# The inverse of the delta rule in blocks of 64 tokens on two quadrants of TensorE

## The reference

```python
def chunk_gated_delta(q, k, v, beta, g):      # CHUNK = 64, 4 heads, dk = dv = 128
    ...
    L = jnp.where(strict, jnp.einsum('bhnid,bhnjd->bhnij', kb, k) * gamma, 0.0)
    rhs = jnp.concatenate([v * beta[..., None], kb * jnp.exp(gc)[..., None]], axis=-1)
    sol = lax.linalg.triangular_solve(jnp.eye(C, dtype=L.dtype) + L, rhs,
                                      left_side=True, lower=True, unit_diagonal=True)
    U, W = sol[..., :dv], sol[..., dv:]
```

## Time and profile before

| | us |
|---|---|
| median of 3 runs (lowest, highest) | 1252.11 (1249.11, 1254.0) |
| the profiled execution, its own time | 1254.81 |
| its span, first to last instruction | 1253.0 |
| PE busy in the span | 1182.9 |
| DVE busy in the span | 671.5 |
| ACT busy in the span | 557.8 |
| mean granted TensorE clock, share of full | 0.982 |

### The profile page before, as it was taken

The page is one execution under the profiler, slowest core; times in us unless marked ns, Lnnn a source line. Parts: engine busy times, 40 slices in busy tenths (PEclk is TensorE's granted clock), DMA queues, the critical chain, the costliest instruction groups (busy, mean ns, idle before and its releaser), DMA issues.

```text
span 1253.0 us, 15678 instructions
## 1 busy us (share of the span) xinstructions
PE 1182.9 (94%) x6279; PEld 876.6 (70%) x6279; DVE 671.5 (54%) x720; ACT 557.8 (45%) x633; POOL 46.2 (4%) x90
## 2 busy tenths in 40 slices
PE   5999989999998999889998999999999989999986
PEld 5989868888887977677844848638658458477351
DVE  4866665444454433478804857408668048484053
ACT  3771344343434376356704636307447046354041
POOL 7000000000000022000000000000000000000000
PEclk8999999999998999989999999999999999999999
DMA  9622139655553432248989999999999899998993
GB/s 313 181 101 69 35 123 379 223 199 170 189 178 131 153 135 75 86 144 317 331 325 421 419 420 421 367 421 420 417 384 419 329 421 419 410 413 318 421 417 125
DMA packets 116926, 352.07 MB, mean 281 GB/s; under 512 B 8096, under 2 KB 55216, under 8 KB 116848
## 3 DMA queue, kind: packets, MB, share of 16 engines
q1 hardware_dynamic: 115552, 347.11, 72.2%
q0 software_dynamic: 1296, 3.90, 1.0%
HBM read 349.93 MB, written 1.05 MB: 280 GB/s over the span
## 4 chain that ended last, share of the span: by engine, by line
PE 85%; DMA 6%; DVE 5%; ACT 3%; issue 1%; SPq 0%; DVEq 0%; ACTq 0%
PE ps L547 20%; PE ps L548 19%; PE ps L549 19%; PE ps L1584 8%; PE ps L1605 6%; DMA arena_c<-in_o_moe_w_dram 4%; PE ps L1529 2%; PE ps L1566 2%; DVE all_lo L1755 1%; DMA arena_a<-in_o_moe_w_dram 1%; PE ps L1541 1%; PE ps L1290 1%; DMA arena_a<-in_e_w_in_dram 1%; PE ps L1448 1%; PE ps L1285 1%
## 5 line engine op out<-in xcount | busy, mean ns | idle before, releaser
L1755 DVE TENSOR_TENSOR all_lo<-arena_c,all_hi 128x1408 fp32r<-128x1408 f32 (+1 forms) x120 | 170.7, 1448 | 215.8 <-ACT all_hi L794 215.5
L794 ACT ACTIVATE all_hi<-arena_c 128x1408 fp32r<-128x1408 f32 (+1 forms) x120 | 146.5, 1247 | 242.9 <-DMA arena_c<-in_o_moe_w_dram 196.9
L1755 DVE TENSOR_TENSOR all_lo<-arena_a,all_hi 128x1408 fp32r<-128x1408 f32 (+1 forms) x96 | 138.4, 1471 | 23.8 <-ACT all_hi L794 23.4
L547 PE MATMUL ps<-all_hi,xg_hi 128*128 128x512 f32 (+1 forms) x384 | 145.2, 378 | 2.9 <-ACT u_act L1037 2.9
L548 PE MATMUL ps<-all_lo,xg_hi 128*128 128x512 f32 (+1 forms) x384 | 144.4, 376 | 0.0
L794 ACT ACTIVATE all_hi<-arena_a 128x1408 fp32r<-128x1408 f32 (+1 forms) x96 | 119.2, 1262 | 55.1 <-PE ps L549 35.2
L549 PE MATMUL ps<-all_hi,xg_lo 128*128 128x512 f32 (+1 forms) x384 | 143.7, 374 | 0.0
L547 PE MATMUL ps<-all_hi,x_hi 128*128 128x512 f32 (+1 forms) x336 | 126.2, 376 | 4.2 <-DVE all_lo L1748 2.3
L1748 DVE TENSOR_TENSOR all_lo<-arena_a,all_hi 128x2048 fp32r<-128x2048 f32 x40 | 91.4, 2290 | 62.1 <-ACT all_hi L787 62.1
L548 PE MATMUL ps<-all_lo,x_hi 128*128 128x512 f32 (+1 forms) x336 | 122.9, 366 | 0.0
L549 PE MATMUL ps<-all_hi,x_lo 128*128 128x512 f32 (+1 forms) x336 | 122.7, 365 | 0.0
(11 more groups left out here) (350 smaller groups left out, 1820.6 us busy)
## 6 DMA issues: line engine op xcount, KB each, us to landing
arena_c<-in_o_moe_w_dram SPq DMA_DIRECT2D x136, 704.0 KB, 9.3
arena_a<-in_o_moe_w_dram SPq DMA_DIRECT2D x120, 704.0 KB, 9.0
arena_c<-in_o_moe_w_dram SPq DMA_DIRECT2D x45, 1024.0 KB, 14.5
arena_a<-in_o_moe_w_dram SPq DMA_DIRECT2D x35, 1024.0 KB, 15.6
arena_c<-in_e_ffn_w_dram SPq DMA_DIRECT2D x36, 512.0 KB, 4.8
arena_a<-in_e_ffn_w_dram SPq DMA_DIRECT2D x30, 512.0 KB, 5.1
arena_a<-in_e_w_in_dram SPq DMA_DIRECT2D x24, 512.0 KB, 8.8
arena_a<-in_o_w_qkv_dram SPq DMA_DIRECT2D x12, 512.0 KB, 4.2
```

The lines of the kernel that those rows point to most:

```text
L547: pe.matmul(o, a_hi, b_hi, start=first, stop=False)
L794: act.activation(unit(all_hi, st), in_ring(WHERE[v][0] + off, st.size), ACT.Copy).then_inc(hi_done, 1)
L1755: tt(unit(all_lo, st), in_ring(WHERE[v][0] + off, st.size), unit(all_hi, st).bitcast(F32), ALU.subtract).then_inc(lo_done, 1)
```

## The change

Levels 0 to 5 never connect the first 64 tokens of a unit with the last 64, so X, X transposed and T are block diagonal until level 6. The change keeps only the two 64x64 diagonal blocks, each on its own partitions, packed to 64 columns per unit. Every matmul of 128x128x128 becomes two of 64x64x64: one with rows 0 to 63 of the array into partitions 0 to 63, one with rows 64 to 127 into partitions 64 to 127 of the same bank. DVE's instructions shrink from 128x512 to 128x256. At level 5 the last subtraction writes the two blocks into `inv_all`, 128 columns per unit, with one instruction for each half of the partitions. The last level becomes two corner products per unit, with a plain copy and a multiplication by -1 on DVE, 64 partitions each. `inv_all` then takes the place of `inv_xt` in the solve. POOL copies the masks into packed form once the convolution no longer needs the memory, and sets the unused corner of `inv_all` to zero; it builds one mask less at the start. The fillers keep their places.

```diff
-    LEVELS = 7
+    LEVELS = 6
...
+            pool.wait_ge(conv_done, 6)
+            for rows in HALVES:
+                pool.tensor_copy(half_masks[rows, 0:LEVELS, :], level[rows, 0:LEVELS, rows])
+                pool.tensor_copy(half_masks[rows, LEVELS, :], ident[rows, rows])
+            pool.memset(inv_all[HALVES[1], :, HALVES[0]], 0.0)
+            pool.drain().then_inc(masks_ready, 1)
...
+            def in_halves(bank, hf, a, b):
+                for m in range(4):
+                    u = 4 * hf + m
+                    for rows in HALVES:
+                        last = mm(ps[rows, bank, m * CH:(m + 1) * CH], a(u, rows), b(u, rows), start=True, stop=True)
+                return last
...
-                    for m in range(4):
-                        u = 4 * hf + m
-                        last = mm(ps[:, hf, m * P:(m + 1) * P], lower[:, u, :], inv_x[:, u, :] if k else ident[:, :],
-                                  start=True, stop=True)
-                    last.then_inc(t_done, 1)
+                    in_halves(hf, hf, lambda u, rows: lower[rows, u, rows], x_part_of if k else unit_of).then_inc(t_done, 1)
+                fill(k)
...
-                    if 0 < k < LEVELS - 1:
...
+                        in_halves(6 + hf, hf, xt_part_of, t_part_of).then_inc(x_done, 1)
+                    in_halves(2 + hf, hf, t_part_of, xt_part_of if k else unit_of).then_inc(xt_done, 1)
+            first, second = HALVES
+            for hf in range(2):
+                pe.wait_ge(x_ready, 2 * LEVELS + hf - 1)
+                for m in range(4):
+                    u = 4 * hf + m
+                    last = mm(ps[second, hf, m * CH:(m + 1) * CH], lower[first, u, second], inv_x[first, u, :], start=True, stop=True)
+                last.then_inc(t_done, 1)
+            fill(LEVELS)
+            for hf in range(2):
+                pe.wait_ge(t_ready, 2 * LEVELS + hf + 1)
+                pe.wait_ge(xt_ready, 2 * LEVELS + hf - 1)
+                for m in range(4):
+                    u = 4 * hf + m
+                    last = mm(ps[first, 2 + hf, m * CH:(m + 1) * CH], inv_t[second, u, :], inv_all[second, u, second],
+                              start=True, stop=True)
+                last.then_inc(xt_done, 1)
             gate_mix()
...
-                last = mm(two(0)[:, u * P:(u + 1) * P], kbe[:, u, :], inv_xt[:, u, :], start=True, stop=True)
+                last = mm(two(0)[:, u * P:(u + 1) * P], kbe[:, u, :], inv_all[:, u, :], start=True, stop=True)
...
+            vec.wait_ge(masks_ready, 1)
             for k in range(LEVELS):
...
-                    tt(inv_t[:, us, :], ps[:, hf, :].rearrange("p (u n) -> p u n", u=4), units4(level[:, k, :]),
-                       ALU.mult).then_inc(t_ready, 1)
+                    tt(inv_t[:, us, :], units_of(hf), units4(half_masks[:, k, :]), ALU.mult).then_inc(t_ready, 1)
...
+                    if k < LEVELS - 1:
+                        tt(inv_xt[:, us, :], old_xt, units_of(2 + hf), ALU.subtract).then_inc(xt_ready, 1)
+                    else:
+                        for rows in HALVES:
+                            ins = tt(inv_all[rows, us, rows], old_xt[rows], units_of(2 + hf)[rows], ALU.subtract)
+                        ins.then_inc(xt_ready, 1)
...
+            for hf in range(2):
+                us = slice(4 * hf, 4 * hf + 4)
+                vec.wait_ge(t_done, 2 * LEVELS + hf + 1)
+                vec.tensor_copy(inv_t[second, us, :], units_of(hf)[second]).then_inc(t_ready, 1)
+            for hf in range(2):
+                us = slice(4 * hf, 4 * hf + 4)
+                vec.wait_ge(xt_done, 2 * LEVELS + hf + 1)
+                ts(inv_all[first, us, second], units_of(2 + hf)[first], -1.0, None, ALU.mult).then_inc(xt_ready, 1)
             gate_out()
```

More of the change, by code:

```diff
@@ L275, in trunk @@
         level_at = nc.sbuf_base
-        level = sb("level", [P, LEVELS, P])
+        level = sb("level", [P, LEVELS + 1, P])
         iota = sb("iota", [P, P])
@@ L315, in trunk @@
         rows_raw = kd[:, 0, :]
[L316 to L318 removed]
+        inv_at = conv_in[:, :, :].rearrange("p a b -> p (a b)")
+        inv_x, inv_xt, inv_t = (inv_at[:, k * U * CH:(k + 1) * U * CH].rearrange("p (u n) -> p u n", u=U) for k in range(3))
+        inv_all = inv_at[:, 3 * U * CH:3 * U * CH + U * P].rearrange("p (u n) -> p u n", u=U)
+        half_at = 3 * U * CH + U * P
+        half_masks = inv_at[:, half_at:half_at + (LEVELS + 1) * CH].rearrange("p (k n) -> p k n", n=CH)
+        HALVES = (slice(0, CH), slice(CH, P))
         vb = xn[:, 0, :].rearrange("p (u n) -> p u n", u=U)
@@ L392, in trunk @@
         back = put("back", [SLOTS, TILES, P])
-        assert end[0] <= level_at + 4 * LEVELS * P
+        assert end[0] <= level_at + 4 * (LEVELS + 1) * P
         y_exp = over(gain_at + 4 * D)[0]("y_exp", [SLOTS, D])
@@ L1274, in _, with x_part_of, xt_part_of, t_part_of @@
                     (project_N if i < 10 else project_T)(i, 4 + i % 2, [half])
+            def in_halves(bank, hf, a, b):
[4 more added lines that the diff above has]
+                return last
+            def x_part_of(u, rows):
+                return inv_x[rows, u, :]
+            def xt_part_of(u, rows):
+                return inv_xt[rows, u, :]
+            def t_part_of(u, rows):
+                return inv_t[rows, u, :]
+            def unit_of(u, rows):
+                return ident[rows, rows]
+            for k in range(LEVELS):
+                for hf in range(2):
+                    if k:
+                        pe.wait_ge(x_ready, 2 * k + hf - 1)
+                    in_halves(hf, hf, lambda u, rows: lower[rows, u, rows], x_part_of if k else unit_of).then_inc(t_done, 1)
+                fill(k)
                 if k == 0:
@@ L1296, in _ @@
             for u in range(U):
-                last = mm(two(0)[:, u * P:(u + 1) * P], kbe[:, u, :], inv_xt[:, u, :], start=True, stop=True)
+                last = mm(two(0)[:, u * P:(u + 1) * P], kbe[:, u, :], inv_all[:, u, :], start=True, stop=True)
             last.then_inc(sol_done, 1)
             for u in range(U):
-                last = mm(two(6)[:, u * P:(u + 1) * P], inv_xt[:, u, :], vb[:, u, :], start=True, stop=True)
+                last = mm(two(6)[:, u * P:(u + 1) * P], inv_all[:, u, :], vb[:, u, :], start=True, stop=True)
```

24 lines of the change are left out of this document (11 added, 13 removed).

## The result

The changed kernel takes 1240.13 us (median of 4 runs, 1238.94 to 1241.57) beside 1253.05 for the kernel before (4 runs, 1249.11 to 1255.54): a ratio of 0.9902, 95% interval 0.9887 to 0.9917. The prediction was 1239.5. The profiled execution took 1240.6, with a span of 1238.6.

What follows compares the result with a forecast made beforehand. PE's instruction stream was taken as the bound: 13.2 + 1.8 - 2.1 - 0.3 = 12.6 us less, giving 1242.2 profiled or 1239.5 as median. Forecast's own range 1236.5 to 1242.5, over the cases 1236.5 to 1252.

Steps and rivals of the forecast that it cites:

- PE's stream is the bound and what it saves counts in full: Inverse, 84 to 142 us: PE busy 55.8 of 58 us, so its savings count in full while DVE keeps up.
- A pair in 0.060: Two 64x64x64 records on opposite quadrants take 0.060 us, so 16 groups save 0.83 each, 13.2 us in all.
- The changes of tiling, 0.30 a stretch: Seven tiled stretches on PE's path, each about 0.30 us more for switching tiling; 2.1 us lost.
- The seventh stretch: XT of the last level, in front of `gate_mix`; charged about 0.30 us for tiling like the other stretches.
- The first stretch: XT of level 0 with T of level 1; charged about 0.30 us for changing the tiling.
- The change of tiling into the scores: Existing row-tiled scores: 0.85 us less 0.64 for slots at full overlap, so a tiling change costs 0.2.
- The last level on one quadrant, 0.89 each: Last level's T and XT: 16 unpaired records each at 0.056, 0.89 us saved each, 1.8 together.
- T of level 0 hidden by the wait for `kbe`: T of level 0 would end earlier, but PE then waits for ACT's `kbe` until 87.87 anyway; no gain counted.
- DVE keeps pace; 0.3 for the waits: Inverse: DVE instructions fall to about 0.42 us and keep pace; 0.3 us lost for waits, including 0.8 before level 5.
- POOL's packing and the tail at nothing: POOL's mask packing after the last convolution at 66.4 us costs nothing; the 0.9 gained before `gate_mix` passes through.
- No overlap: Rival: row tiles sharing a PSUM bank do not overlap, a pair takes 0.112 us; 1252.7 us, chance 0.13.
- Feeding: Rival: four instructions per pair set PE's pace; 1245.9 us at 0.085 a pair, about 1252 at 0.109; chance 0.16.
- The clock over the whole stage: Rival: small tiles count as too little work, the granted clock falls in the inverse; about 1274 us, chance 0.08.

Runs made afterwards that it cites:

- probe: Changed kernel plus five rows of extra small matmuls (32 or 64 columns, one quadrant alone, tiling switches) between T of level 0 and filler 0; 1245.72 us, one run.
- kbe_by_bank: Changed kernel with ACT's 16 scaled copies before filler 0 ordered by bank, so filler 0 waits for 4 kbe copies instead of 8; 1238.26 us.
- dve_twice: Changed kernel with each X and XT subtraction of levels 1 to 5 (XT up to level 4) preceded by a copy into spare memory; 1243.72 us.
- the small shapes: The same run as the probe: changed kernel plus five rows of extra small matmuls before filler 0; 1245.72 us, one run.
- banks2: Changed kernel plus extra 64x64x64 matmuls before filler 0: pairs into one bank, two banks, two column tiles, and all four quadrants; 1243.72 us, one run.
- the first experiment: Changed kernel with each half group's four lower-quadrant matmuls issued first, then the four upper ones, instead of alternately; 1242.25 us.
- order: The same run as the first experiment: changed kernel issuing four matmuls per quadrant in turn instead of alternating; 1242.25 us.
- wide_t: Changed kernel with T of levels 1 to 5 again one matmul per unit, 128 weight columns and 64 moving columns; 1243.17 us.
- ln_split: Changed kernel with the second tile's layer norm moved on DVE from behind level 4 to behind the last level's T copies; 1240.55 us.
- both edits: Changed kernel with ACT's copies ordered by bank and the layer norm split; 1235.67 us, and 1235.08 when run again beside the changed kernel's 1239.4.
- the run lengths: Changed kernel plus extra 64x64x64 matmuls before filler 0, in runs of 2, 8 and 16 per quadrant; 1241.29 us, one run.

## Why the prediction was right

The forecast was 12.6 us less and 12.9 came, between the medians; by its own steps:

- **PE's stream is the bound and what it saves counts in full:** right. The chain steps from PE group to PE group but for DVE's layer norm and split subtractions at level 5, and the 13.1 us gained at `gate_mix` are all there at the first output product, 158.46 to 145.38.
- **A pair in 0.060:** 0.058. By starts, X, XT and T of a level took 5.27 us (108.17 to 113.44) and take 2.94 (104.63 to 107.57); 48 pairs at 0.0584 are 2.80, so the groups saved 2.47 against 3x0.83 = 2.49.
- **The changes of tiling, 0.30 a stretch:** 0.14 of the 2.94, and the filler in front of X is 0.10 longer (3.07 against 2.97), 0.24 together. The level's sum is 2.23 where 2.49 - 0.30 = 2.19 was said. The probe's 0.29 for both ways is the same thing without a "before" in it. The seventh stretch was charged too much: XT of the last level saved 0.81, and 0.59 was said, since `gate_mix` had a change of tiling in front of it before as well. The first stretch went the other way, 1.14 where 1.66 - 0.30 = 1.36 was said, so two misses of 0.22 cancel; without either the forecast would still have been near.
- **The change of tiling into the scores:** by the record times of 0.224 and 0.112 the slots at full overlap are 0.67, not 0.64, which leaves 0.18 instead of 0.2; the sum does not change by it.
- **The last level on one quadrant, 0.89 each:** XT's 16 records take 1.07 with the change into `gate_mix`, 16x0.058 and 0.14. A lone record costs 0.058, not 0.056.
- **T of level 0 hidden by the wait for `kbe`:** right, 1.66 became 2.37, and `kbe_by_bank` shows that it was the order of ACT's copies that held it there.
- **DVE keeps pace; 0.3 for the waits:** right in size. Level 5 waits 0.68 (0.8 said, 0.55 before), and 0.18 in front of the last T was not named; together 0.31 more than before. At level 0 XT and T take 2.15 us in the chain (64 records from 90.76), where 32 pairs and the change of tiling are 2.01; DVE's subtraction for T of half 1 ends at 92.18, so the 0.1 that was named is there as well, 0.14. In all 0.45 came where 0.3 was put. `dve_twice` shows how near it is.
- **POOL's packing and the tail at nothing:** POOL packs from 66.40 to 70.3. The first copy takes 2.5 us where its like takes 0.5; DVE's L1786 runs at the same time (66.25 to 68.53), but no run shows that this is the reason. The packing ends 16 us ahead of DVE's first mask instruction at 86.94.
- **The rivals.** No overlap: the small shapes exclude it (a pair takes what one record takes), and `banks2` excludes a cost of the shared bank. Feeding: pairs at 0.03 exclude it. The clock over the whole stage: it stayed at the full level.

What failed was not in the prediction but in the first experiment's expectation: I had taken it that without alternation nothing would overlap, and two thirds of the gain stayed. I also had no step for the 1.3 us behind 187 us in the profile; the medians, 12.9 apart, suggest that they are not the change's.

## What to carry to other kernels

Where a chain of small matmuls is block diagonal, put the blocks on opposite quadrants of the array and issue them alternately: a pair then costs what one costs. It pays only if weight columns and moving columns both shrink, and each change of tiling costs 0.15 us a way. Read the cost of a matmul from start to start in the chain, not from its own duration (220 ns here for 29). And once the bound engine is faster, read its list of waits again: 2.8 us of waiting that had been half hidden were had by reordering two other engines' queues.

## What the hardware showed that I had not expected

**PE's look-ahead is short.** Work for a free quadrant starts only if it stands within about three records of the running one: with runs of 8 records 0.33 us of 0.93 is hidden, with two runs of 32 only 0.17 of 3.87.

**The granted clock falls for some 3 us in some executions.** Busy time by stretch in `order` (columns as in the earlier trace rows), where PE had idled some 2 us before filler 0:

```profile
88.00:91.00 3.00, 3.00 (x16) 2.78 (x14) 0.00 (x0) 0.00 (x0) 0.00 (x0) 0.50 0.02 5
91.00:97.00 6.00, 6.00 (x90) 5.79 (x90) 3.95 (x6) 0.00 (x0) 0.00 (x0) 0.96 0.12 14
```

Three us at 1.2 GHz, in which a product's matmuls stand 0.21 us apart in the chain instead of 0.12: filler 0 takes 4.3 us instead of 3.0. It stood in the profiles of `order`, `wide_t` and `ln_split` (0.64 in 88 to 92), and not in those of the kernel before, the changed kernel or `dve_twice`, although PE idled there as well (1.66 and 2.37 us). In the three profiles in which the wait is 0.3 it was not seen, nor in those of the run lengths (no wait) and the banks (1.86). But the kernel with the small shapes, whose PE did not wait there, has 0.56 in 93 to 96, so the wait is not the only thing that brings it on. The same holds at the first output products, where PE had been half idle: 0.67 in the changed kernel (0.63 before), 1.4 us, and none of it in `ln_split`, both profiles with both edits and the second profile of the changed kernel, which is the same program as the first. So one stage can differ by 1.3 us between two executions with the same waits. The two executions with the highest mean clock, 0.993, are the fastest of their sets: 1249.44 of the nine of the kernel before (median 1253.01) and 1240.14 of `order` (median 1242.25). Whether the clock is part of what both edits gained over the waits they removed is not shown.

**Four quadrants at once.** Four independent records of 64x64x64 take 0.062 us together, one takes 0.058.
